# Four of twelve modulation sums accumulated on GpSimd instead of VectorE

## The chip, the cores and the metric

One core of a Trainium2 chip runs the whole program: two layers of an attention block, then two layers of a modulated mixer block, for 256 tokens of width 2048 in float32. The metric is the device time of one execution in microseconds (us), lower is better.

## What is computed

The change is in the modulation of the second block. Each of its two layers takes a conditioning vector `c` (one row of 2048) and forms shift, scale and gate rows from a 2048 x 6144 matrix; the first layer does the same for the context with `c_ctx`:

```python
def modulation(cond, w, b, n):
    m = jax.nn.silu(cond) @ w[:, :n * D_MODEL] + b[:n * D_MODEL]
    return jnp.split(m, n, axis=-1)

for i in range(DEPTH):                       # DEPTH = 2
    sh, sc, gt = modulation(c_lat, w_ada[i], b_ada[i], 3)
    u = x * (1.0 + sc) + sh
    ...
    y = even_mixer(...) if i % 2 == 0 else odd_mixer(...)
    x = layer_norm(alpha * x + gt * y, ln_g[i], ln_b[i])
```

The even mixer is a gated linear attention with four heads (`gla_chunked`, 256 keys and 256 values per head, forwards and backwards) beside a short convolution; the odd mixer is a projection, window means with a pooled product, and an output projection. Everything is float32 in and out.

## The kernel before

**The weight stream and its split.** All large products are made of float32 weights in 504 blocks of 128 x 1024 (512 KB), loaded in order by SyncE's queue into a ring of four `stage` buffers. ScalarE writes the high part of a block (`wh`, L272), VectorE the rest (`wl<-stage,wh`, L293, one TENSOR_TENSOR), both into rings of four (`SPLITS`), and TensorE does 12 matmuls of 128 x 512 for each block (L340 to L342: high by high, low by high, high by low, for two k-tiles and two token tiles). A block's `stage` buffer is loaded again once `lo_ready` says that VectorE has read it; `wh` and `wl` are written again once `split_free` says that TensorE has used them.

**The modulation beside it.** A product with one row would waste TensorE, so each modulation sum is made as 16 steps: a block of the matrix, 128 x 1024, is brought by GpSimd's queue into `mstage` (three buffers), and one instruction adds it, times a column of `silu(c)`, into one of two accumulators `macc` (the first step of a sum only multiplies, L614, the 15 others are one SCALAR_TENSOR_TENSOR each, L617). TensorE then adds over the partitions with a product by ones, either to columns (`modulation_columns`, L1884) or, for the gates, to rows (`modulation_gate`, L2123). Semaphore `mod_sum` counts the steps; GpSimd issues the load of a unit once the step three units earlier is counted. The first four sums are made for `c` and `c_ctx` together (64 loads and 128 steps, within the first block). The other eight, sums 4 to 11 in the order of `MOD_BLOCK2`, have 16 steps each, called `mod_next(k)` with k from 0 to 127.

**Order.** Every engine's program is written out by hand. VectorE's steps stand between its split instructions:

- k 0 to 63 (sums 4 to 7): in the context projection and the key, value and query projections.
- none in the four heads of the gated linear attention, where VectorE makes the decays of eight levels (L1525 to L1533) and merges their scores (L1513), while TensorE does a weight block beside each level.
- k 64 to 66 directly after the heads, 67 to 74 in `beside_y`, 75 to 78 in the convolution stage, 79 to 95 in the output projection of the even mixer (`OUTE_MODS`; the first of them, 79, ends sum 8), 96 to 127 in the odd mixer's projection (`mod_some`).

Who waits for sums 8 to 11: the gate of the first layer is sums 7 and 8 (`modulation_gate(0, 0)` and `(0, 1)`), sum 9 is turned to columns between the two token tiles of the even output projection's last blocks, and sums 10 and 11 are the gate of the last layer (`modulation_gate(1, 0)` and `(1, 1)`). A new sum may start only when its accumulator is free: sum 8 after the columns of sum 6 (`mod_summed`), sum 9 after `modulation_gate(0, 0)` (`gt_ready` at 2), sum 10 after `modulation_gate(0, 1)` (`gt_ready` at 4), sum 11 after the columns of sum 9.

Of the kernel before, what the change touches and what calls it, by code (L numbers as in the profile page):

```python
# [15 lines left out]
ALU = mybir.AluOpType  # L16
# [7 lines left out]
KT = D // P  # L24
# [65 lines left out]
MOD_BLOCK1 = [(0, True), (2, True), (1, True), (3, True)]  # L90
MOD_BLOCK2 = [(8, False), (9, False), (6, False), (4, False), (5, False), (7, False), (10, False), (11, False)]
# [2 lines left out]
MOD_LAYER = sum(MOD_OPS[0:2])  # L94
MOD_COLS = [0, 2, 4, 6, 8, 9, 10, 11, 12]
MOD_UNITS = 3
WARM_FIRST, WARM_NEXT = 8, 3
OUT_PIECES = [(0, 0, 1024), (0, 1024, 1024), (1, 0, 1024), (1, 1024, 512), (1, 1536, 512)]

# [18 lines left out]
def build(nc, A, out):  # L118
    ctx = ExitStack()
    with ctx:  # L120
        def sb(name, shape, dt=F32):
            return ctx.enter_context(nc.sbuf_tensor(name, shape, dt))
# [4 lines left out]
        def sem(name):  # L127
            return ctx.enter_context(nc.semaphore(name))
# [9 lines left out]
        arena = sb("arena", [P, 15360])  # L138
        mstage = sb("mstage", [P, MOD_UNITS, 2 * COLS])
        macc = sb("macc", [P, 2, 2 * COLS])  # L140
# [7 lines left out]
        scols = sb("scols", [P, 2, KT])  # L148
# [88 lines left out]
        o_ready, o_done = sem("o_ready"), sem("o_done")  # L237
        m_full = [sem(f"mod_full{b}") for b in range(MOD_UNITS)]
        silu_c, mod_sum = sem("silu_c"), sem("mod_sum")
        mod_summed, mod_cols = sem("mod_summed"), sem("mod_cols")  # L240
# [3 lines left out]
        def once(name):  # L244

            if name not in made:
                made[name] = sem(name)
            return made[name]
# [16 lines left out]
        block = ctx.enter_context(nc.Block())  # L265
# [335 lines left out]
        def mod_op(dve, l, i, o, both, half=0):  # L601

            n = o // 2 if both else o
            w = 1 - o % 2 if both else half
            unit = KT * (2 * l + i) + n
            block, acc, col = mstage[:, unit % MOD_UNITS, :], macc[:, w, :], scols[:, 1 - o % 2 if both else 0, n:n + 1]
            if not both or o % 2 == 0:
                dve.wait_ge(m_full[unit % MOD_UNITS], 16 * (unit // MOD_UNITS + 1))
            if n == 0:
                if i in (9, 10):  # L610
                    dve.wait_ge(once("gt_ready"), 2 if i == 9 else 4)
                else:
                    dve.wait_ge(mod_summed, 2 * l + i + 1 if i < 5 else i if i < 9 else 9)
                nc.vector.tensor_scalar(acc, block, col, None, ALU.mult).then_inc(mod_sum, 1)  # L614
            else:
                dve.wait_ge(mod_sum, mod_done(l, i) + o - (1 if both else 0))
                nc.vector.scalar_tensor_tensor(out=acc, in0=block, scalar=col, in1=acc, op0=ALU.mult,  # L617
                                               op1=ALU.add).then_inc(mod_sum, 1)
# [10 lines left out]
        @block.gpsimd  # L629
        def _(pool):  # L630
            nc.gpsimd.memset(ones[:], 1.0).then_inc(k_ready, 1)

            others = [(tab[:, 0:768], A["att_tab"]), (rope_t, A["rope"]), (bcols[:], A["bcols"]),
                      (sinks[:], A["sinks"].partition_broadcast(P)), (rcnt[:], A["rcnt"])]
            pool.wait_ge(full[3], 16)
            done = []
            for cp, both in MOD_SEQ:
                for n in range(KT):
                    unit = len(done)
                    if unit == MOD_UNITS:  # L640
                        for dst, src in others:
                            pool.dma_start(dst, src).then_inc(tables_loaded, 16)
                    if unit >= MOD_UNITS:
                        pool.wait_ge(mod_sum, done[unit - MOD_UNITS])
                    k = n % KPB
                    pool.dma_start(mstage[:, unit % MOD_UNITS, :].rearrange("p (c n) -> p c n", c=2),  # L646
                                   WM[n // KPB, :, 2 * cp:2 * cp + 2, COLS * k:COLS * k + COLS])\
                        .then_inc(m_full[unit % MOD_UNITS], 16)
                    done.append((done[-1] if done else 0) + (2 if both else 1))


        @block.scalar
# [473 lines left out]
        def _(dve):  # L1126
# [241 lines left out]

            def mod_next(k):

                i = len(MOD_BLOCK1) + k // KT
                mod_op(dve, 0, i, k % KT, False, half=i % 2)

# [76 lines left out]
            for m in range(16):  # L1450
                n = 4 * (m // 8) + m % 4
# [28 lines left out]
            for hd in range(GH):  # L1480
# [9 lines left out]
                for d, dst in ((0, PF), (1, SB_)):  # L1490
                    n = 8 + 2 * hd + d
# [25 lines left out]
                for v, b in enumerate(LEVELS + [P, None]):  # L1517
                    k = 9 * hd + v
# [343 lines left out]
        def _(pe):  # L1862
# [494 lines left out]
            def turn_quad(q, t):  # L2357

                pe.wait_ge(once("ln_first"), 2 * t + q + 1)
                _, m = u.take()  # L2360
                turned(pe, m - 2)
                for j in range(4):
                    a = P * (4 * q + j)
                    last = nc.tensor.transpose(quad(m)[0][:, P * j:P * j + P], X[:, t, a:a + P], ident[:])
                last.then_inc(tp_ready, 1)
                uses.append(u.n)
# [182 lines left out]
```

## Time and profile before

| | |
|---|---|
| three runs, median (lowest to highest) | 1728.97 us (1727.98 to 1729.22) |
| the profiled execution, its own time | 1727.48 us |
| its span in the trace | 1725.7 us |
| TensorE's mean granted clock | 0.99 of full |
| busy: TensorE, VectorE, ScalarE, GpSimd | 98%, 77%, 52%, 8% |
| moved from HBM and back | 385 MB and 4 MB, 226 GB/s over the span |

The profiled execution lies 1.5 us under the median of the three runs. Busy time of an engine is the sum of its instructions' durations; for TensorE the ends are modelled, so that its 98% does not mean peak speed. GpSimd's 8% is the issuing of transfers, 0.72 us for each. Times of stretches are given in us from the start of the span: the four heads are at 998 to 1203, the rest of the even mixer's products up to the convolution at 1203 to 1290, the end of the convolution and the even output projection at 1290 to 1396, the odd mixer's projection at 1410 to 1600.

### The profile page before, as it was taken

To read this page: it belongs to the slowest core of one execution; us is meant where nothing else is said; L and a number is where in the kernel's file an instruction comes from. 1 tells how busy PE (TensorE), PEld (TensorE's weight loads), DVE (VectorE), ACT (ScalarE), POOL (GpSimd) and SP (SyncE) were. 2 spreads that over 40 slices of the span, in tenths; PEclk is the share of its full clock that TensorE was granted. 3 is DMA by queue.
4 is the path that set the end of the run, shared out by engine and by line. 5 is a ranking of instruction groups with operands and counts; after the bars stand their busy time and mean duration, and the time that the engine had idled before them with its cause. 6 is when DMAs were issued, how large, how long until landed. Compare 5 with 4: busy or idle time off the path is not lost.

```text
span 1725.7 us, 22328 instructions
## 1 busy us (share of the span) xinstructions
PE 1684.4 (98%) x8100; PEld 1393.9 (81%) x8100; DVE 1336.4 (77%) x1805; ACT 890.8 (52%) x1353; POOL 142.0 (8%) x202
## 2 busy tenths in 40 slices
PE   9999999999999999999999999999999999999996
PEld 7888888888888888878877878778777778878885
DVE  7978878879778878687966877778876978667766
ACT  6447564455465734555844456655534364444432
POOL 1100000001000000011211200000101101110000
PEclk9999999999999999999999999999999999999998
DMA  8856545658655545689977933334959869887663
GB/s 322 328 200 205 173 160 160 205 192 305 230 183 183 173 156 195 236 279 357 336 253 228 359 118 122 123 123 147 326 183 332 306 233 318 280 260 228 223 203 111
DMA packets 110466, 390.60 MB, mean 226 GB/s; under 512 B 16204, under 2 KB 17116, under 8 KB 108732
## 3 DMA queue, kind: packets, MB, share of 16 engines
q1 hardware_dynamic: 74944, 268.99, 44.6%
q0 software_dynamic: 27856, 101.19, 19.0%
q10 hardware_dynamic: 7566, 19.08, 3.1%
q8 instruction: 64, 1.05, 0.3%
q14 instruction: 36, 0.29, 0.0%
HBM read 385.02 MB, written 4.19 MB: 226 GB/s over the span
## 4 chain that ended last, share of the span: by engine, by line
PE 84%; DVE 8%; ACT 4%; issue 2%; DMA 2%; ACTq 0%; SPq 0%; DVEq 0%
PE L L340 23%; PE L L342 23%; PE L L341 23%; PE TP L444 3%; DVE wl L293 2%; DMA stage<-in_w_stream 1%; PE AB L1884 1%; PE AB L1976 1%; ACT wh L272 1%; PE TP L1989 1%; PE AB L2281 1%; PE AB L2212 1%; PE AB L1979 1%; DVE arena L1525 1%; PE AB L1980 1%
## 5 line engine op out<-in xcount | busy, mean ns | idle before, releaser
L340 PE MATMUL L<-wh,xth 128*128 128x512 f32 (+1 forms) x1948 | 788.6, 405 | 8.7 <-DVE wl L293 5.9
L293 DVE TENSOR_TENSOR wl<-stage,wh 128x1024 fp32r<-128x1024 f32 x504 | 612.0, 1220 | 228.1 <-ACT wh L272 227.1
L272 ACT ACTIVATE wh<-stage 128x1024 fp32r<-128x1024 f32 x504 | 530.0, 1057 | 495.3 <-PE L L342 352.8
L342 PE MATMUL L<-wh,xtl 128*128 128x512 f32 (+1 forms) x1948 | 762.1, 391 | 0.0
L341 PE MATMUL L<-wl,xth 128*128 128x512 f32 (+1 forms) x1948 | 761.0, 391 | 0.0
L340 PEld LDWEIGHTS L<-wh,xth 128*128 128x128 f32 x1948 | 368.3, 189 | 86.4 <-DVE wl L293 10.2
L342 PEld LDWEIGHTS L<-wh,xtl 128*128 128x128 f32 x1948 | 367.8, 189 | 78.3
L341 PEld LDWEIGHTS L<-wl,xth 128*128 128x128 f32 x1948 | 368.6, 189 | 74.5 <-issue 4.1
L617 DVE SCALAR_TENSOR_TENSOR macc<-mstage,scols,macc 128x1024 f32<-128x1024 f32 x240 | 306.8, 1278 | 4.8 <-DMA mstage<-in_w_mod 4.0
L646 POOL DMA_DIRECT2D mstage<-in_w_mod x192 | 138.9, 723 | 1435.8 <-DVE macc L617 1002.3
L716 ACT ACTIVATE pa<-pa,st 128x128 f32<-128x128 f32 x96 | 43.1, 450 | 71.3 <-DVE st L1227 36.5
L949 ACT ACTIVATE arena<-arena 128x256 f32<-128x256 f32 (+1 forms) x136 | 48.1, 424 | 47.9 <-DVE arena L1533 47.8
L728 ACT ACTIVATE pa<-TP 128x384 f32<-128x384 f32 x48 | 23.5, 490 | 68.7 <-PE TP L1989 68.7
L444 PE MATMUL TP<-ident,arena 128*128 128x128 f32 x344 | 49.2, 275 | 1.3 <-DVE xtl L478 1.0
L444 PEld LDWEIGHTS TP<-ident,arena 128*128 128x128 f32 x344 | 41.9, 143 | 10.2 <-issue 2.5
L1218 DVE SCALAR_TENSOR_TENSOR pa<-tab,AB 128x384 f32<-128x384 f32 x48 | 26.5, 552 | 24.2 <-PE AB L1980 18.9
L1247 DVE SCALAR_TENSOR_TENSOR arena<-AB,st,arena 128x64 f32<-128x64 f32 (+1 forms) x96 | 25.0, 302 | 19.1 <-PE AB L2002 18.1
L691 ACT ACTIVATE arena<-L,st 128x512 f32<-128x512 f32 (+1 forms) x60 | 37.5, 678 | 2.0 <-PE L L342 1.9
L466 ACT ACTIVATE xth<-TP 128x512 fp32r<-128x512 f32 x40 | 23.1, 588 | 22.5 <-PE TP L444 22.5
L478 DVE TENSOR_TENSOR xtl<-TP,xth 128x512 fp32r<-128x512 f32 x40 | 27.0, 684 | 6.5 <-ACT xth L466 6.5
L2265 PEld LDWEIGHTS AB<-arena 128*128 128x128 f32 x160 | 19.9, 191 | 12.2 <-issue 6.0
L2265 PE MATMUL AB<-arena 128*128 128x128 f32 x160 | 22.2, 282 | 6.6 <-DVE arena L1493 4.8
(233 smaller groups left out, 1325.8 us busy)
## 6 DMA issues: line engine op xcount, KB each, us to landing
stage<-in_w_stream SPq DMA_DIRECT2D x504, 512.0 KB, 4.7
mstage<-in_w_mod POOLq DMA_DIRECT2D x192, 512.0 KB, 6.3
arena<-in_ctx ACTq DMA_DIRECT2D x1, 2048.0 KB, 12.9
x_kept<-X ACTq DMA_DIRECT2D x1, 2048.0 KB, 9.9
X<-x_kept ACTq DMA_DIRECT2D x1, 2048.0 KB, 11.7
arena<-in_b_ada ACTq DMA_DIRECT2D x2, 1024.0 KB, 11.3
arena<-in_ln_g ACTq DMA_DIRECT2D x2, 1024.0 KB, 9.8
X<-in_x SPq DMA_DIRECT2D x3, 512.0 KB, 8.7
```

What stands on the lines that cost most here:

```text
L272: nc.scalar.activation(wh[:, s % SPLITS].rearrange("p a b -> p (a b)"), stage[:, s % RING, :], ACT.Copy).then_inc(hi_ready, 1)
L293: nc.vector.tensor_tensor(wl[:, s % SPLITS].rearrange("p a b -> p (a b)"), stage[:, s % RING, :], wh[:, s % SPLITS].rearrange("p a b -> p ...
L340: nc.tensor.matmul(o, xh, w[0], start=start, stop=False, skip_group_check=True)
L341: nc.tensor.matmul(o, xh, w[1], start=False, stop=False, skip_group_check=True)
L342: last = nc.tensor.matmul(o, xl, w[0], start=False, stop=True, skip_group_check=True)
L444: last = nc.tensor.transpose(bank[0:width, j, t * P:t * P + P], src(t), ident[:])
L617: nc.vector.scalar_tensor_tensor(out=acc, in0=block, scalar=col, in1=acc, op0=ALU.mult, op1=ALU.add).then_inc(mod_sum, 1)
L646: pool.dma_start(mstage[:, unit % MOD_UNITS, :].rearrange("p (c n) -> p c n", c=2), WM[n // KPB, :, 2 * cp:2 * cp + 2, COLS * k:COLS * k + ...
L691: ins = nc.scalar.activation(dst(t), L[bank][:, t, 0:width], fn, scale=scale(t))
L716: ins = nc.scalar.activation(pr[b][:, a:a + w], pr[b][:, a:a + w], ACT.Exp, bias=ngm[:, 2 * b + t:2 * b + t + 1], scale=1.0 if swa else ML ...
L949: return nc.scalar.activation(dst, src, ACT.Exp, scale=1.0 / 16)
L2265: last = nc.tensor.matmul(bank[:, P * j:P * j + P], ks[:, dc, P * j:P * j + P], qs[:, dc, P * i:P * i + P], start=dc == 0, stop=dc == 1)
```

## The change

Steps k of 64 and above (sums 8 to 11) are left out of VectorE's program. GpSimd makes each of them with two instructions instead of one: it multiplies the staged block by its column in place, waits for that, and adds it to the accumulator (the first step of a sum multiplies straight into the accumulator). Its own steps stand in its program ahead of the load that needs their buffer. The places where TensorE waits, the buffers, and all loads are the same.

```diff
+POOL_MODS = 64
...
+            def pool_step(k, done):
+
+                i, n = len(MOD_BLOCK1) + k // KT, k % KT
+                unit = 4 * KT + k
+                block, acc, col = mstage[:, unit % MOD_UNITS, :], macc[:, i % 2, :], scols[:, 0, n:n + 1]
+                pool.wait_ge(m_full[unit % MOD_UNITS], 16 * (unit // MOD_UNITS + 1))
+                if n == 0:
+                    if i in (9, 10):
+                        pool.wait_ge(once("gt_ready"), 2 if i == 9 else 4)
+                    else:
+                        pool.wait_ge(mod_summed, i if i < 9 else 9)
+                pool.wait_ge(mod_sum, done[unit - 1])
+                if n == 0:
+                    nc.gpsimd.tensor_scalar(acc, block, col, None, ALU.mult).then_inc(mod_sum, 1)
+                else:
+                    nc.gpsimd.tensor_scalar(block, block, col, None, ALU.mult).then_inc(once("mod_scaled"), 1)
+                    pool.wait_ge(once("mod_scaled"), k - POOL_MODS - (k - POOL_MODS) // KT)
+                    nc.gpsimd.tensor_tensor(acc, acc, block, ALU.add).then_inc(mod_sum, 1)
...
+                    step = unit - 4 * KT - MOD_UNITS
+                    if step >= POOL_MODS:
+                        pool_step(step, done)
                     if unit >= MOD_UNITS:
                         pool.wait_ge(mod_sum, done[unit - MOD_UNITS])
...
+            for step in range(len(MOD_BLOCK2) * KT - MOD_UNITS, len(MOD_BLOCK2) * KT):
+                pool_step(step, done)
...
             def mod_next(k):
 
+                if k >= POOL_MODS:
+                    return
                 i = len(MOD_BLOCK1) + k // KT
```

GpSimd's program before, from its tables to its end (`stage_full3` is the first weight blocks' arrival, `mod_sum` the count of steps made):

```order
L631 MEMSET ones 128x128
L646 DMA mstage<-in_w_mod 128x2x512 [waits stage_full3]
L646 DMA mstage<-in_w_mod 128x2x512 x2
L642 DMA tab<-in_att_tab 128x768
L642 DMA rcnt<-in_rcnt 128x8
L646 DMA mstage<-in_w_mod 128x2x512 [waits mod_sum] x189
```

And now, from the last row before its steps on (lines are those of the changed program, in which L669 is the load; `mod_full` is the arrival of a unit in each of the three buffers, `mod_scaled` counts the scalings):

```order
L669 DMA mstage<-in_w_mod 128x2x512 [waits mod_sum] x128
L649 ISA
L649 TENSOR_SCALAR macc<-mstage,scols 128x1024 [waits mod_sum,mod_summed,mod_full2]
L669 DMA mstage<-in_w_mod 128x2x512 [waits mod_sum]
L651 TENSOR_SCALAR mstage<-mstage,scols 128x1024 [waits mod_sum,mod_full0]
L653 TENSOR_TENSOR macc<-macc,mstage 128x1024 [waits mod_scaled]
```

After 131 loads GpSimd alternates between a step (scaling and addition) and a load. The first of its steps waits for the columns of sum 6 and for nothing in the heads.

VectorE's program before, from the last instruction of the last head (L1515) on:

```order
L1515 COPY pa<-AB 128x256 [waits at_added,lv_ready]
L293 TENSOR_TENSOR wl<-stage,wh 128x1024 [waits hi_ready] x4
L614 TENSOR_SCALAR macc<-mstage,scols 128x1024 [waits mod_summed,mod_full2]
L617 SCALAR_TENSOR_TENSOR macc<-mstage,scols,macc 128x1024 [waits mod_sum,mod_full0]
L617 SCALAR_TENSOR_TENSOR macc<-mstage,scols,macc 128x1024 [waits mod_sum,mod_full1]
L538 TENSOR_SCALAR st<-st 128x8 [waits stat_sum]
L541 RECIPROCAL st<-st 128x8 [waits stat_sd]
L293 TENSOR_TENSOR wl<-stage,wh 128x1024 [waits hi_ready]
L617 SCALAR_TENSOR_TENSOR macc<-mstage,scols,macc 128x1024 [waits mod_sum,mod_full2]
```

And now (L294 is the split, which was L293, and L1542 the copy):

```order
L1542 COPY pa<-AB 128x256 [waits at_added,lv_ready]
L294 TENSOR_TENSOR wl<-stage,wh 128x1024 [waits hi_ready] x4
L539 TENSOR_SCALAR st<-st 128x8 [waits stat_sum]
L542 RECIPROCAL st<-st 128x8 [waits stat_sd]
L294 TENSOR_TENSOR wl<-stage,wh 128x1024 [waits hi_ready] x5
L1587 SCALAR_TENSOR_TENSOR arena<-arena,st,pa 128x256 [waits stat_rs,gla_w]
```

The steps between the splits are gone; the splits and all else stand in their old order, in this stretch and in the later ones.

## Rows read from the trace of the kernel before

**Rows 1.** The page: engines' busy time, then costly groups and issues.

```profile
PE 1684.4 (98%) x8100; PEld 1393.9 (81%) x8100; DVE 1336.4 (77%) x1805; ACT 890.8 (52%) x1353; POOL 142.0 (8%) x202
L617 DVE SCALAR_TENSOR_TENSOR macc<-mstage,scols,macc 128x1024 f32<-128x1024 f32 x240 | 306.8, 1278 | 4.8 <-DMA mstage<-in_w_mod 4.0
mstage<-in_w_mod POOLq DMA_DIRECT2D x192, 512.0 KB, 6.3
```

**Rows 2.** Busy time by stretch; behind POOL: granted clock, DMA share, GB/s.

```profile
998.00:1203.00 205.00, 196.87 (x1005) 163.06 (x1004) 169.44 (x306) 123.60 (x222) 0.45 (x1) 0.99 0.36 118
1203.00:1290.00 87.00, 85.28 (x363) 66.99 (x362) 65.59 (x66) 41.79 (x58) 8.22 (x12) 1.00 0.75 257
1290.00:1396.00 106.00, 101.92 (x458) 81.95 (x458) 83.93 (x88) 40.10 (x44) 14.45 (x20) 1.00 0.90 319
1410.00:1600.00 190.00, 190.00 (x841) 153.28 (x840) 137.69 (x126) 91.83 (x113) 20.96 (x29) 1.00 0.82 270
```

**Rows 3.** VectorE in order of time, one level of the second head.

```profile
1067.66 1.21 DVE L293 TENSOR_TENSOR wl<-stage,wh 128x1024 fp32r<-128x1024 f32 x1
1069.22 0.42 DVE L1525 TENSOR_TENSOR arena<-arena 128x256 f32<-128x256 f32 x1
1070.51 0.68 DVE L1529 TENSOR_TENSOR arena<-arena 128x512 f32<-128x512 f32 x1
1071.78 1.22 DVE L293 TENSOR_TENSOR wl<-stage,wh 128x1024 fp32r<-128x1024 f32 x1
```

**Rows 4.** TensorE in order of time, the same level's matmuls and the next's.

```profile
1067.79 1.05 PE L2265 MATMUL AB<-pa 128*128 128x128 f32 x8
1071.42 1.05 PE L2265 MATMUL AB<-arena 128*128 128x128 f32 x8
```

**Rows 5.** GpSimd in order of time: last load before, first after the heads.

```profile
989.42 0.72 POOL L646 DMA_DIRECT2D mstage<-in_w_mod  x1 [1.99 <-DVE macc L617]
1202.55 0.72 POOL L646 DMA_DIRECT2D mstage<-in_w_mod  x1 [212.40 <-DVE macc L614]
```

**Rows 6.** When the columns of sum 6 are read, and VectorE's first level.

```profile
996.99 0.17 DVE L624 SCALAR_TENSOR_TENSOR mcols<-AB,bcols 128x8 f32<-128x8 f32 x1 [2.04 <-PE AB L1884]
1009.73 0.42 DVE L1525 TENSOR_TENSOR arena<-arena 128x256 f32<-128x256 f32 x1 [1.08 <-ACT arena L949]
```

**Rows 7.** The modulation instructions on VectorE by stretch.

```profile
1203.00:1290.00 87.00, 13.45 (x11) 1.00 0.75 257
1290.00:1396.00 106.00, 24.30 (x19) 1.00 0.90 319
1396.00:1600.00 204.00, 38.35 (x30) 0.99 0.78 258
```

**Rows 8.** TensorE's waits, 1203 to 1290 (first row) and 1290 to 1405.

```profile
PE L L340 <- DVE wl L293: 1.3, 1, 1.3
...
PE L L340 <- DVE wl L293: 3.0, 2, 1.8
PE L L340 <- DVE xtl L1752: 2.7, 1, 2.7
PE TP L444 <- DVE xtl L478: 1.0, 1, 1.0
```

**Rows 9.** GpSimd's own instructions on data, all at the start.

```profile
L631 POOL MEMSET ones<- 128x128 f32 x1 | 0.2, 204 | 0.3 <-POOLq L2537 0.3
L2537 POOL MEMSET const-float32-0.0<- 128x1 f32 x1 | 0.1, 93 | 0.3 <-issue 0.3
```

**Rows 10.** The split's durations: min, median, max over all 504.

```profile
L293 DVE TENSOR_TENSOR wl<-stage,wh x504: 1193/1220/1229, 8.0 to 1702.9; 128x1024 fp32r<-128x1024 f32 x168
```

**Rows 11.** The chain that ended last, 1290 to 1651, of longer pieces.

```profile
1289.13 1.72 PE AB L2123 x4
...
1307.59 12.27 DMA stage<-in_w_stream
...
1322.37 12.73 DMA stage<-in_w_stream
...
1345.49 1.72 PE AB L2123 x4
1393.49 1.68 PE AB L1884 x16
...
1635.60 1.72 PE AB L2123 x4
1650.97 1.72 PE AB L2123 x4
```

## The prediction

> **What bounds the kernel now.** I read the page first. TensorE is busy for 98% of the span and VectorE for 77% [rows 1]. That says only that VectorE's relief is worth little on the whole; what it is worth is settled in the stretches where instructions leave or come. So next the busy times by stretch [rows 2], then TensorE's waits there [rows 8], then the order of time in the heads [rows 3, 4], where the change brings a new user of time.
>
> In the stretches that lose VectorE work (1203 to 1600) TensorE hardly waits for VectorE: 1.3 us up to 1290, then 3.0 us for the split, 2.7 us and 1.0 us for other instructions up to 1405 [rows 8]; from 1410 to 1600 it is busy for 190.0 of 190 us [rows 2]. In the heads it is otherwise. One level takes VectorE from 1067.66 to 1071.78, 4.12 us, and in it every instruction stands right behind the last [rows 3]. TensorE's part of a level needs 3.63 us (1067.79 to 1071.42, in a level where its blocks were ready) [rows 4]. So within the levels VectorE sets the pace and has 0.49 us too much per level: anything that holds VectorE there holds the kernel.
>
> **The change, part by part.**
>
> Removed from VectorE: 64 steps, 60 of them at 1278 ns [rows 1] and four cheaper first steps, together 13.5, 24.3 and 38.4 us in the three stretches [rows 7], 76.1 us (of them 0.7 us for each first step is not counted by that line). What of it lies on the path is bounded by what TensorE waits: at most 1.3 + 3.0 + 1.0 = 5.3 us of [rows 8] can go, since the 2.7 us end a chain of ScalarE and VectorE work without a step in it. The 3.0 us have a second cause: in 1290 to 1396 the chain holds two weight loads of 12.27 and 12.73 us [rows 11] while the transfers run at 319 GB/s with the DMA engines busy for 0.90 [rows 2]. Sum 8's 16 loads, 8 MB, move into the heads, where they run at 118 GB/s, so the pressure at 1203 to 1290 falls, but at 1290 to 1396 GpSimd still wants 16 to 19 loads where 20 were issued. I take a gain of **2 us**, between 0 and 5.3.
>
> Added to GpSimd: 64 scalings and 60 additions of 128 x 1024, and their waits. No row shows such an instruction. The nearest are two memsets: 204 ns for 128 columns and 93 ns for one [rows 9], 0.87 ns per column, hence 0.98 us for one stream of 1024 columns. A scaling is one stream in and one out: 0.98 us if they overlap, 1.87 us if not. An addition has two in: 1.87 us if only the output overlaps, 2.77 us if nothing does. I take 1.0 us for the scaling, by the memset, and the middle, 2.3 us, for the addition: 3.3 us per step (ends 2.85 and 4.6 us). The Trainium skill (GPSIMD Engine Reference, Performance versus the Vector engine) gives 4497 ns for an addition of 2048 float32 columns, thus an estimate of 2.25 us for 1024; no row here shows it, and with it the sum below would be the same to a few us.
>
> Moved: sum 8. Before, GpSimd waited 212.40 us, all through the heads, for VectorE's first step of it [rows 5]. Now its steps need only the columns of sum 6, which are there at 997.0 [rows 6]. So 16 scalings and 15 additions run in the heads. Nobody needs the sum before 1345 [rows 11]. The cost of this part is nothing if GpSimd and VectorE do not disturb each other, and at most the whole time of GpSimd's instructions, 16 x 1.0 + 15 x 2.3 = 50.5 us, if one stops while the other reads. The trace can't decide between them: GpSimd's 192 load issues leave the split's duration as it is (1193 to 1229 ns in all 504) [rows 10], but they read no tile. I take the upper kind: both engines read 128-partition tiles of the same memory, and an engine either has its own way to them or takes turns; a middle needs a special reason. The Trainium skill (SBUF — State Buffer, Who interferes with whom) states just this: a VectorE instruction with two SBUF inputs contends with a GpSimd instruction that reads SBUF, and whoever comes second is fully blocked. No run here shows it yet; by that rule the forecast stands, without it the first rival.
>
> With turns, a step takes GpSimd 3.3 us, 0.72 us for its load issue [rows 5], and about 0.5 us before each of the two while a VectorE instruction of 0.42 to 1.22 us [rows 3] ends: some 5 us, of which VectorE has 1.8 us. From 997.0 to the first level at 1009.73 [rows 6] go 2.5 steps, mostly beside VectorE's waits. The other 13.5 fall into levels that are full: 13.5 x 3.3 = 44.6 us. The 13.5 x 1.8 us of VectorE work done meanwhile are 6 levels, whose slack of 0.49 us gives back 3 us. Heads: **+42 us**, and 0 at the other end, or 60 us with 4.6 us per step. The loads cost nothing: a unit is asked for two steps ahead, 10 us, and lands in 6.3 us [rows 1].
>
> Between 1203 and 1290 GpSimd stands, since sum 9 waits for the gate product at 1289 [rows 11].
>
> From 1290 to 1396: sum 9. GpSimd's tiles take 50.5 us; VectorE keeps 83.9 - 25.0 (19 steps and a first one) = 59 us [rows 2, 7], most of it the 33 splits: 109 us wanted where there are 106. The splits have a lead of some blocks, but a split that comes late also puts off the next weight load, and those are on the chain here [rows 11]. I take +8 us, between -3 and +22.
>
> From 1396 to 1600: sums 10 and 11. GpSimd's tiles take 101 us; VectorE keeps 98 of 190 us (137.7 less the 30 steps and two first ones) [rows 2, 7]. With turns that are 1 us longer beside splits, a step takes 6.5 us: 32 of them end near 1396 + 208 = 1604 plus what was lost, and the gate wants them at 1636 and 1651 [rows 11]. TensorE has a lead of three blocks here. I take 0, and +15 if GpSimd's step is of the long kind.
>
> Sum: -2 + 42 + 8 = **+48 us** on the profiled execution's 1727.5 us, which is 1775 us; the median of the runs shown is 1.5 us above that execution, which does not matter at this size.
>
> **Rivals.**
>
> 1. *No disturbance: faster.* If the two engines read side by side, VectorE's levels stay at 4.12 us, and only the gain is left: 2 us, up to 5.3. Time 1724 us (1721 to 1729). It decides by a point that the sum gives: the loss outweighs the gain as soon as GpSimd holds VectorE for over 5.3 / 50.5, a tenth, of its own instructions' time in the heads. For it speaks that nothing in the trace shows a disturbance; against it, that the loss needs so little. Chance 0.20.
>
> 2. *GpSimd is late.* With 4.6 us per step, or if GpSimd is the one that is mostly blocked, sum 9 needs 16 x 7.5 = 120 us where 106 are, and TensorE waits at the columns at 1393 [rows 11] for 14 us; sums 10 and 11 need 240 us from there and are late for the gates by some 10 us more. If it is late by long instructions that hold VectorE too, the heads add 60: 1727.5 + 60 + 24 + 10 = 1821 us. Chance 0.12. If it is GpSimd alone that is held, only its lateness counts, about 1750 us: chance 0.08, together with a half disturbance (a slower rate instead of turns), which gives the same +24.
>
> 3. *The change does less than it says:* sum 8 does not run in the heads. Its waits are met at 997 [rows 6], so I give that nothing of its own.
>
> **How the numbers follow.** Forecast 0.60 (1755 to 1800), rival 1 0.20, late and long 0.12, held or half 0.08. A measurement of this kernel tells about 0.2%, 3.5 us, from no change. Rival 1 lies across that border: 0.12 faster, 0.08 same. All else is slower: 0.80. The range for 8 in 10 has to reach from the edge of rival 1 to the lower part of the long case: 1726 to 1812 us.
>
> **What would show it.** In the changed profile: GpSimd's scaling near 1.0 us and addition near 2.3 us when alone; in the heads 16 of each but one, from 997 on; the split and the level instructions there longer than 1.22 and 0.42 to 0.68 us, or gaps between them, as long as GpSimd works, and levels of 4.12 us as soon as it has ended; the first head longer by some 40 us and the last unchanged. From 1410 on splits that are longer without TensorE waiting. The prediction is wrong if the levels beside GpSimd's steps keep 4.12 us (rival 1), or if TensorE waits at the columns of sum 9 or at the last gate (rival 2).

## The result and the profile after

The changed kernel takes 1776.63 us (median of 4 runs, 1772.02 to 1782.21) against 1728.47 us before (1726.06 to 1729.22): 1.028 times, interval 1.0263 to 1.0297. It is 48 us slower. Its profiled execution has a span of 1773.7 us, 48.0 us over the 1725.7 us before.

First the page of the changed kernel: busy time, and the groups that answer to [rows 1]; behind the bar busy us, mean ns of one, and the idle time before them. L294 is the split (L293 before).

```profile
PE 1701.7 (96%) x8100; PEld 1404.9 (79%) x8100; DVE 1374.8 (78%) x1741; ACT 891.3 (50%) x1353; POOL 509.1 (29%) x326
...
L294 DVE TENSOR_TENSOR wl<-stage,wh 128x1024 fp32r<-128x1024 f32 x504 | 673.8, 1347 | 230.9 <-ACT wh L273 229.3
...
L618 DVE SCALAR_TENSOR_TENSOR macc<-mstage,scols,macc 128x1024 f32<-128x1024 f32 x180 | 230.0, 1278 | 6.4 <-DMA mstage<-in_w_mod 6.0
L651 POOL TENSOR_SCALAR mstage<-mstage,scols 128x1024 f32<-128x1024 f32 x60 | 192.8, 3214 | 2.9 <-POOL macc L653 0.3
L653 POOL TENSOR_TENSOR macc<-macc,mstage 128x1024 f32<-128x1024 f32 x60 | 158.7, 2644 | 5.0
```

VectorE makes 60 of these instructions fewer and is busy for 38 us more. Its records have grown: an instruction that is held back counts as busy. The split's mean went from 1220 to 1347 ns, while its shortest is still 1192 ns.

The next view is VectorE in order of time within the first head, one level of the changed kernel, to be read against [rows 3]; columns are start, duration, engine, line, operation.

```profile
1023.24 1.21 DVE L294 TENSOR_TENSOR wl<-stage,wh 128x1024 fp32r<-128x1024 f32 x1
1024.38 0.44 DVE L1540 COPY_PREDICATED pa<-tab,AB 128x256 f32<-128x256 uint32 x1
1024.80 0.92 DVE L1552 TENSOR_TENSOR arena<-arena 128x256 f32<-128x256 f32 x1
1025.64 0.41 DVE L1553 TENSOR_TENSOR arena<-arena 128x256 f32<-128x256 f32 x1
1025.98 0.68 DVE L1555 TENSOR_TENSOR arena<-arena 128x512 f32<-128x512 f32 x1
1026.58 0.68 DVE L1556 TENSOR_TENSOR arena<-arena 128x512 f32<-128x512 f32 x1
1027.18 0.41 DVE L1559 TENSOR_TENSOR arena<-arena 128x256 f32<-128x256 f32 x1
1027.52 2.60 DVE L1560 TENSOR_TENSOR arena<-arena 128x256 f32<-128x256 f32 x1
1030.04 1.21 DVE L294 TENSOR_TENSOR wl<-stage,wh 128x1024 fp32r<-128x1024 f32 x1
```

And GpSimd in the same time:

```profile
1023.33 0.77 POOL L669 DMA_DIRECT2D mstage<-in_w_mod  x1 [0.30 <-POOL macc L653]
1024.14 3.03 POOL L651 TENSOR_SCALAR mstage<-mstage,scols 128x1024 f32<-128x1024 f32 x1
1027.25 2.58 POOL L653 TENSOR_TENSOR macc<-macc,mstage 128x1024 f32<-128x1024 f32 x1
1030.13 0.77 POOL L669 DMA_DIRECT2D mstage<-in_w_mod  x1 [0.30 <-POOL macc L653]
```

L1560 wants 0.42 us. It starts 0.27 us after GpSimd's addition and ends at 1030.12, 0.29 us after the addition's end at 1029.83: held for nearly all of it. L1552 meets the scaling and is 0.92 us long in place of 0.43; but L1553 to L1556 run at full speed while the scaling goes on until 1027.17. A level takes 6.80 us (1023.24 to 1030.04) against 4.12 us: 2.2 us for the addition, 0.5 us for the scaling.

How much a scaling costs depends on when VectorE's instruction comes. In the second head the same L1556 starts just behind a scaling and takes 1.64 us in place of 0.68:

```profile
1092.09 2.86 POOL L651 TENSOR_SCALAR mstage<-mstage,scols 128x1024 f32<-128x1024 f32 x1
1092.12 1.64 DVE L1556 TENSOR_TENSOR pa<-arena 128x512 f32<-128x512 f32 x1
```

If it needs its usual 0.68 us once it is let in, it was let in 1.0 us after the scaling's start (an estimate from these two rows: 1092.12 + 1.64 - 0.68 - 1092.09). The same working over the whole profile, for the 34 scalings that were not lengthened themselves: all 13 splits and level instructions that started in their first 0.98 us were held, and let in 0.98 to 1.02 us after the scaling's start; none of the 34 that started later was held. In the additions that were not lengthened the 24 held instructions were let in 2.19 to 2.30 us after the start. So a scaling keeps these instructions out for about the first 1.0 us of its 2.86, an addition for about 2.3 of its 2.4 us. The page calls GpSimd's spans rough, but these numbers hardly vary.

In the levels of the second head the scaling costs 1.0 us so, and the addition 1.7 us (L1552 takes 2.17 us); a level takes 6.8 us again. TensorE waits for the levels (first the two rows of the changed kernel, then the same two of the kernel before):

```profile
PE AB L2292 <- DVE pa L1556: 16.2, 10, 2.9
PE AB L2292 <- DVE arena L1556: 7.3, 11, 1.4
...
PE AB L2265 <- DVE arena L1529: 1.7, 9, 0.2
PE AB L2265 <- DVE pa L1529: 1.0, 5, 0.2
```

(TensorE's waits over the whole execution: us in total, times, longest.) Not every instruction of VectorE is held. In the view by line, which gives min/median/max in ns, those with two inputs in the on-chip memory have long ones; those that read the matmuls' memory (`TP`, `AB`, `L`) and at most one tile of the on-chip memory have none, nor has the memset:

```profile
L1560 DVE TENSOR_TENSOR arena<-arena x32: 410/417/2605, 1016.1 to 1224.8; 128x256 f32<-128x256 f32 x32
...
L1540 DVE COPY_PREDICATED pa<-tab,AB x28: 430/440/450, 1024.4 to 1225.2; 128x256 f32<-128x256 uint32 x28
...
L1515 DVE MEMSET arena<- x4: 485/485/485, 1001.4 to 1188.1; 128x512 f32 x4
...
L479 DVE TENSOR_TENSOR xtl<-TP,xth x40: 676/682/692, 239.2 to 1677.5; 128x512 fp32r<-128x512 f32 x40
...
L1697 DVE TENSOR_TENSOR arena<-L,arena x8: 678/682/693, 1370.1 to 1443.4; 128x512 f32<-128x512 f32 x8
```

The Trainium skill (SBUF — State Buffer, Who interferes with whom) says that an instruction with two SBUF inputs contends with a GpSimd instruction that reads SBUF and that one with at most one, outside VectorE's two-port modes, does not: these rows agree, with 2605 ns beside 417 and 450 beside 440. For how long they contend is another matter, as the scaling shows.

To place the 48 us I use one ruler for all kernels, the starts of the same instructions: the first and the fourth head's scaling of queries (L1486 before), the first gate product, the last product for the columns of sum 9, the last low part of the turned tiles at the start of the odd mixer (L1752 before), the last gate product, and the end. Lengths in us between them, each from one profiled execution; the part ahead of the heads varies from 995.6 to 1003.2 us in all these executions and is left out.

| kernel | heads 1 to 4 | to the gate | sum 9 | between the mixers | odd mixer | end |
|---|---|---|---|---|---|---|
| before | 158.3 | 132.8 | 105.9 | 18.6 | 238.6 | 73.6 |
| changed | 187.4 | 132.8 | 113.0 | 25.3 | 241.7 | 73.6 |
| e1, sum 8 only | 187.1 | 132.7 | 102.0 | 20.3 | 238.5 | 73.6 |
| e2, sums 9 to 11 | 156.7 | 132.8 | 136.8 | 24.3 | 242.0 | 73.6 |
| e3, sums 10 and 11 | 158.1 | 132.9 | 105.4 | 24.1 | 241.7 | 73.6 |
| e4, VectorE's steps narrow | 158.9 | 132.8 | 104.8 | 17.4 | 238.6 | 73.6 |
| e5, scalings alone | 161.7 | 132.7 | 115.5 | 20.9 | 239.4 | 73.6 |
| e6, additions alone | 190.8 | 132.8 | 138.6 | 32.6 | 250.2 | 73.5 |
| e7, writes alone | 158.8 | 132.8 | 104.4 | 19.1 | 238.6 | 73.6 |
| e8, GpSimd's steps narrow | 158.1 | 132.8 | 107.2 | 18.8 | 238.5 | 73.6 |
| e9, sum 11 only | 159.0 | 132.8 | 104.5 | 17.4 | 238.7 | 73.6 |
| e10, sum 10 late | 189.0 | 132.8 | 114.9 | 20.6 | 245.1 | 73.5 |
| e11, additions apart | 185.4 | 132.7 | 112.5 | 25.3 | 250.4 | 73.6 |

The changed kernel loses 29.1 us in the heads (19.9 in the first, 9.3 in the second, nothing in the third), 7.1 with sum 9, 6.7 between the mixers and 3.1 in the odd mixer: 46.0 us, and 2.0 us lie ahead of the heads.

With sum 9 TensorE stands before the columns for 2.8 us and then works at half the clock, so that the product itself takes 3.57 us in place of 1.68 [rows 11]. Its timeline there, in the changed kernel:

```profile
1426.74 0.39 PE L343 MATMUL L<-wh,xtl 128*128 128x512 f32 x1
1429.90 3.57 PE L1911 MATMUL AB<-ones,macc 128*128 128x1 f32 x16 [2.77 <-POOL macc L653]
1433.34 0.77 PE L341 MATMUL L<-wh,xth 128*128 128x512 f32 x1
```

GpSimd's last addition for the sum, the 15th, ended at 1429.85; it had started the sum at 1322.16, 6.7 us per step. Between the mixers, VectorE normalizes in a chain that TensorE waits for. The view is VectorE in order of time:

```profile
1438.77 2.16 DVE L1724 SCALAR_TENSOR_TENSOR st<-moments,st 128x1 f32<-128x1 f32 x1
1440.97 2.46 DVE L1772 TENSOR_SCALAR X<-X,st 128x512 f32<-128x512 f32 x2
```

In the kernel before these were 0.16 and 1.00 us:

```profile
1399.20 0.16 DVE L1697 SCALAR_TENSOR_TENSOR st<-moments,st 128x1 f32<-128x1 f32 x1
1399.40 1.00 DVE L1745 TENSOR_SCALAR X<-X,st 128x512 f32<-128x512 f32 x2
```

One column costs 2 us when it meets an addition (GpSimd's record: 1437.86 to 1440.92). The pair on `X` meets a scaling: its second instruction takes 2.00 us and starts at 1441.43, while GpSimd still issues a load (1441.21 to 1441.98); the scaling's record begins at 1442.02, and the instruction is let in 0.9 us after that, by the working above. So it was held from before the record of what holds it.

TensorE has little to do meanwhile, and its clock falls. First the stretch with the product for sum 9's columns, then the stretches after the norm, of the changed kernel (busy time of TensorE, its weight loads, VectorE, ScalarE, GpSimd, then granted clock, DMA share, GB/s):

```profile
1429.90:1433.50 3.60, 3.60 (x17) 3.60 (x18) 1.60 (x4) 0.00 (x0) 3.31 (x2) 0.50 0.51 159
...
1441.10:1445.10 4.00, 1.77 (x8) 1.13 (x8) 3.93 (x5) 2.14 (x5) 3.76 (x3) 0.80 0.49 157
1445.10:1449.10 4.00, 1.10 (x3) 0.94 (x4) 3.79 (x7) 2.95 (x7) 3.66 (x3) 0.50 0.04 6
1449.10:1453.10 4.00, 4.00 (x11) 3.07 (x10) 3.96 (x6) 1.64 (x3) 3.92 (x2) 0.50 0.83 242
```

0.50 is the lower level, 1.2 GHz; in the last stretch TensorE is busy throughout and does 11 matmuls where it does some 20 at the upper level. In the kernel before, the clock falls here too, but less: 0.64 from 1403 to 1407 us and 0.94 in the next 4 us.

### The profile page after: what moved, and what is told of

Same layout as the page of the kernel before. It is cut to its first block, busy times and chain, and to the rows that moved or that the text cites. A ratio compares the mean times of both kernels' runs of the same rounds, so it can differ in the third digit from the quotient of the medians.

```text
span 1773.7 us, 22391 instructions
## 1 busy us (share of the span) xinstructions
PE 1701.7 (96%) x8100; PEld 1404.9 (79%) x8100; DVE 1374.8 (78%) x1741; ACT 891.3 (50%) x1353; POOL 509.1 (29%) x326
## 4 chain that ended last, share of the span: by engine, by line
PE 69%; issue 14%; DVE 7%; POOL 6%; ACT 3%; DMA 1%; ACTq 0%; DVEq 0%; POOLq 0%
PE L L341 19%; PE L L343 19%; PE L L342 19%; POOL mstage L651 3%; PE TP L445 3%; POOL macc L653 2%; PE AB L1911 1%; PE AB L2003 1%; DVE wl L294 1%; DVE arena L1560 1%; DMA arena<-in_w_gate 1%; PE TP L2016 1%; DVE arena L1552 1%; PE AB L2239 1%; ACT wh L273 1%
## 5 line engine op out<-in xcount | busy, mean ns | idle before, releaser
L294 DVE TENSOR_TENSOR wl<-stage,wh 128x1024 fp32r<-128x1024 f32 x504 | 673.8, 1347 | 230.9 <-ACT wh L273 229.3
L669 POOL DMA_DIRECT2D mstage<-in_w_mod x192 | 141.8, 739 | 913.1 <-DVE macc L618 708.7
L618 DVE SCALAR_TENSOR_TENSOR macc<-mstage,scols,macc 128x1024 f32<-128x1024 f32 x180 | 230.0, 1278 | 6.4 <-DMA mstage<-in_w_mod 6.0
L651 POOL TENSOR_SCALAR mstage<-mstage,scols 128x1024 f32<-128x1024 f32 x60 | 192.8, 3214 | 2.9 <-POOL macc L653 0.3
L653 POOL TENSOR_TENSOR macc<-macc,mstage 128x1024 f32<-128x1024 f32 x60 | 158.7, 2644 | 5.0
L649 POOL TENSOR_SCALAR macc<-mstage,scols 128x1024 f32<-128x1024 f32 x4 | 12.8, 3189 | 223.5 <-issue 216.4
L1272 DVE SCALAR_TENSOR_TENSOR arena<-AB,st,arena 128x64 f32<-128x64 f32 (+1 forms) x96 | 25.0, 302 | 19.1 <-PE AB L2029 18.1
L2292 PE MATMUL AB<-pa 128*128 128x128 f32 x128 | 21.0, 314 | 16.3 <-DVE pa L1556 16.2
```

Source lines behind the costliest of these rows:

```text
L294: nc.vector.tensor_tensor(wl[:, s % SPLITS].rearrange("p a b -> p (a b)"), stage[:, s % RING, :], wh[:, s % SPLITS].rearrange("p a b -> p ...
L651: nc.gpsimd.tensor_scalar(block, block, col, None, ALU.mult).then_inc(once("mod_scaled"), 1)
L653: nc.gpsimd.tensor_tensor(acc, acc, block, ALU.add).then_inc(mod_sum, 1)
```

## The experiments

The theory: GpSimd and VectorE take turns at reading, and this costs time where TensorE waits for VectorE soon. Rivals: the loss comes from GpSimd being late for TensorE; from the new order of loads and waits; from any GpSimd work on tiles, reading or not.

**e1: sum 8 alone on GpSimd.** In the changed kernel:

```diff
-                    if step >= POOL_MODS:
+                    if POOL_MODS <= step < POOL_MODS + KT:
...
-                if k >= POOL_MODS:
+                if POOL_MODS <= k < POOL_MODS + KT:
                     return
+                if k == POOL_MODS + KT:
+                    dve.wait_ge(mod_sum, mod_done(0, 9))
```

and without the last loop over `pool_step`.

> GpSimd makes sum 8 alone, in the heads; VectorE makes sums 9 to 11 as before. Theory (the two engines take turns, and the heads pay because VectorE is full there): in the change's profile the starts of the first and the fourth head lie 29 us further apart than before, so this kernel is 27 to 31 us above the kernel before, 1755 to 1760 us, and everything from the end of the heads on has its old length. Rival (most of the 48 us come after the heads, from GpSimd being late for TensorE): under 1745 us.

Measured 1755.95 us, 1.0149 (1.0133 to 1.0165) times before. The heads are 28.8 us longer; of the rest, sum 9's stretch is 3.9 us shorter and the one between the mixers 1.7 us longer in this profile. The largest part of the loss is this one sum in the heads.

**e2 and e3: sums 9 to 11, and 10 and 11, on GpSimd.**

```diff
-POOL_MODS = 64
+POOL_MODS = 80
```

and 96 for e3.

> VectorE makes sum 8 as before, GpSimd sums 9 to 11, so nothing of GpSimd runs in the heads. Theory: the heads are as before, and what is left of the change's 48 us is 17 to 19 us, 1744 to 1748 us; with the run of sum 8 alone the two add up to the change's. Rival (late for TensorE): 30 us or more are left here, over 1757 us.

> VectorE makes sums 8 and 9, GpSimd 10 and 11 alone. In the change's profile the stretch in which sum 9 runs is 7 us longer than before and TensorE waits 6 us in it for GpSimd's last addition at the columns. If that wait is all that stretch costs, this kernel is 7 us under the run of sums 9 to 11, at 1737 to 1741 us, and the rest, 9 to 12 us, is VectorE held in the odd projection. Rival (sums 10 and 11 cost nothing, since TensorE sets the pace there): 1728 us, as before.

e2 gave 1771.19 us, 1.0247 (1.0231 to 1.0262): 23 us over the range expected; the rival's number is met. Its waits of TensorE say why:

```profile
PE AB L1911 <- POOL macc L653: 28.3, 1, 28.3
```

(The profiled execution has a time of 1763.62 us, 7.6 us under the median, so the table holds less than the whole loss.) In e2 GpSimd may start sum 9 only once VectorE has ended sum 8, and that is far on in the output projection:

```profile
1309.93 2.85 POOL L649 TENSOR_SCALAR macc<-mstage,scols 128x1024 f32<-128x1024 f32 x1
```

There are 24.8 us from the gate product (1285.1) to this; in the changed kernel 2.1 us (1320.1 to 1322.16). The heads are as before (156.7), and sum 9's stretch is 30.9 us longer. So the parts don't add: with sum 8 out of the way early, GpSimd just about meets the columns, and without that it is the bound. e3 gave 1737.46 us, 1.0047 (1.0032 to 1.0062), 9.3 us over its kernel before: 5.5 us between the mixers and 3.1 in the odd mixer. That lies in the range expected, but not by the reasoning given for it: e3 is 34 us under e2 and not 7, and most of its loss is in the stretch between the mixers. The 6 us that the expectation names for the wait at the columns are 2.8 us of the matmuls and 3.2 us of the weight loads, which pass side by side; TensorE stood for 2.8 us.

**e4: what the relief of VectorE is worth.** In the kernel before, in `mod_op`:

```diff
+            if unit >= 8 * KT:
+                block, acc = block[:, 0:8], acc[:, 0:8]
```

> The kernel before, with VectorE's steps of sums 8 to 11 made on 8 of the 1024 columns: VectorE is relieved of 64 steps, nothing goes to GpSimd, loads and waits stay. The other 1016 columns of these sums are left out. This is the most that the move can give. The prediction took 2 us of it, at most 5.3: 1723 to 1728 us. If it gives over 8 us, the gain was undersized and the loss with it.

Measured 1729.66 us, 0.9998 (0.9989 to 1.0008): nothing, and just over the range expected. Taking the 64 steps from VectorE gives no time where they stand.

**e5 to e8: which part of a step costs.** In `pool_step`, e5 keeps the scaling of a step without the addition, e6 the addition without the scaling; e7 has five memsets in place of both, e8 cuts every step to 8 columns. First e8's edit, then e7's:

```diff
+                block, acc = block[:, 0:8], acc[:, 0:8]
```

```diff
-                    nc.gpsimd.tensor_scalar(block, block, col, None, ALU.mult).then_inc(once("mod_scaled"), 1)
-                    pool.wait_ge(once("mod_scaled"), k - POOL_MODS - (k - POOL_MODS) // KT)
-                    nc.gpsimd.tensor_tensor(acc, acc, block, ALU.add).then_inc(mod_sum, 1)
+                    for m in range(5):
+                        nc.gpsimd.memset(block, 0.0).then_inc(once("mod_scaled"), 1)
+                        pool.wait_ge(once("mod_scaled"), 5 * (k - POOL_MODS - (k - POOL_MODS) // KT - 1) + m + 1)
+                    pool.sem_inc(mod_sum, 1)
```

> The change without its 60 additions (they are left out; the scalings in place, the loads and all waits stay). In the change's profile a level instruction of VectorE that meets a scaling is about 0.5 us longer, one that meets an addition 2.2 us. Theory (a scaling keeps VectorE out for a part of its 2.86 us only, an addition for all of its 2.4 us): the heads are 8 to 15 us longer, 1734 to 1745 us in all. Rival (each GpSimd instruction keeps VectorE out for its whole time): 16 x 2.86 = 46 us in the heads, over 1765 us. Other rival (only additions disturb): 1728 us.

> The change without its 60 scalings in place: the block is added as it is (the scaling is left out). Theory: 15 additions of 2.4 us in the heads, each holding VectorE for about 2.2 us, 30 us there, and a few after: 1758 to 1768 us. If the two parts simply add, this and the run with scalings alone together lose about the change's 48 us. Rival (the scaling is the costly half): under 1745 us.

> In place of each scaling and addition GpSimd makes five memsets of the same block (the sums are left out), by the 0.98 us estimated for one about 5 us of GpSimd time per step, as long as scaling and addition, but nothing is read. Theory (what they take turns for is reading): the level instructions in the heads keep 0.42 and 0.68 us, 1726 to 1731 us. Rival (any GpSimd work on tiles holds VectorE): 1770 us or more.

> The change with every GpSimd step made on 8 of the 1024 columns: the same instructions, waits, loads and order, and hardly any reading (the other 1016 columns of these sums are left out). Theory (the 48 us are the time of the two instructions' reading, and the lateness that comes from their length): as before, 1724 to 1731 us. Rival (the new order of loads, the extra waits or the code that GpSimd loads costs something): over 1735 us.

e7: 1728.59 us, 0.9998 (0.9983 to 1.0012). GpSimd is busy beside the levels as in the change, with 300 memsets of 0.96 us, and VectorE does not notice:

```profile
L652 POOL MEMSET mstage<- 128x1024 f32 x300 | 287.9, 960 | 14.3 <-POOLq L654 0.4
```

e8: 1729.23 us, 1.001 (0.9997 to 1.0022), with the same instructions, loads and waits as the change. So neither writing nor the order costs. What is left is the part that both runs lack: GpSimd's reading of 1024 columns. Since e8 also moves sum 8's loads into the heads, as the change does, it shows too that the whole move, without that reading, gains nothing.

e5: 1747.02 us, 1.0108 (1.0086 to 1.013), 2 us over the range expected. The heads lose 3.4 us, less than I expected; most of the loss is with sum 9 (9.6 us), where TensorE waits 9.6 us for late splits, 3.0 us before. Without additions a step takes 4 us instead of 6.7, so that 27 scalings fall into that stretch, 17 in the change. VectorE and GpSimd in e5, one level and one step:

```profile
1027.95 1.21 DVE L294 TENSOR_TENSOR wl<-stage,wh 128x1024 fp32r<-128x1024 f32 x1
1029.09 0.45 DVE L1538 COPY_PREDICATED pa<-tab,AB 128x256 f32<-128x256 uint32 x1
1029.50 0.92 DVE L1550 TENSOR_TENSOR arena<-arena 128x256 f32<-128x256 f32 x1
...
1032.55 1.21 DVE L294 TENSOR_TENSOR wl<-stage,wh 128x1024 fp32r<-128x1024 f32 x1
```

```profile
1028.37 3.50 POOL L651 TENSOR_SCALAR mstage<-mstage,scols 128x1024 f32<-128x1024 f32 x1
```

The scaling is 3.50 us long instead of 2.86 (it waits for the split, which ends at 1029.16), and L1550 loses 0.5 us in it; all later instructions of the level run free. L1550 is let in at 1029.99, 1.0 us after the scaling would have started by its length: the same 1.0 us as in the change.

e6: 1820.66 us, 1.0532 (1.0511 to 1.0552). This is the great miss: 92 us, more than scalings and additions together. Its heads lose 32.5 us, as expected; but the stretch of sum 9 loses 32.7, and the two after it 25.6. A part of this is pace: without scalings a step takes 3.4 us, sum 10 starts before sum 9's stretch has ended, and 30 additions fall into it, 15 in the change. TensorE waits 20.8 us for splits there. In the heads one sees how closely the additions stand:

```profile
1020.56 2.35 POOL L651 TENSOR_TENSOR macc<-macc,mstage 128x1024 f32<-128x1024 f32 x1
1023.21 0.72 POOL L667 DMA_DIRECT2D mstage<-in_w_mod  x1 [0.30 <-POOL macc L651]
1023.95 2.38 POOL L651 TENSOR_TENSOR macc<-macc,mstage 128x1024 f32<-128x1024 f32 x1
```

```profile
1016.67 3.40 DVE L1553 TENSOR_TENSOR arena<-arena 128x512 f32<-128x512 f32 x1
1020.00 3.47 DVE L1554 TENSOR_TENSOR arena<-arena 128x512 f32<-128x512 f32 x1
1023.39 3.23 DVE L1557 TENSOR_TENSOR arena<-arena 128x256 f32<-128x256 f32 x1
```

Each of these three instructions of VectorE takes nearly a whole period of 3.4 us, though the addition is 2.4 us long. L1554 starts at 1020.00, while GpSimd still issues a load (1019.81 to 1020.53) and 0.56 us before the addition's record begins, and yet it is held.

**e11: additions alone, apart from the loads.** The load's issue is followed by a memset of 8 columns of a tile of its own, for whose end the addition waits. Against the changed kernel:

```diff
-                    nc.gpsimd.tensor_scalar(block, block, col, None, ALU.mult).then_inc(once("mod_scaled"), 1)
+                    nc.gpsimd.memset(mark[:], 0.0).then_inc(once("mod_scaled"), 1)
```

> The run with additions alone, with a memset of 8 columns between the issue of the load and the addition, whose end the addition waits for (the scalings are left out). In the run with additions alone only one instruction of VectorE gets through per 3.4 us, though an addition takes 2.4 us: theory, the next addition takes the read side while the load is still being issued. Then this run lets VectorE through for some 0.7 us more per step, VectorE's instructions beside it are held for 2.4 us at most in place of 2.8, and the time falls from 1820.7 us to 1785 to 1805 us. Rival (the gap of a load's issue is lost to VectorE for another reason): 1815 us or more.

Measured 1781.11 us, 1.0306 (1.0291 to 1.0322), 40 us less than e6, for two extra things to do per step: a little more than expected. The split now gets through in the gap at full speed, and the held ones are 2.1 to 2.6 us long:

```profile
1018.30 2.60 DVE L1560 TENSOR_TENSOR arena<-arena 128x256 f32<-128x256 f32 x1
1020.82 0.41 DVE L1561 TENSOR_TENSOR arena<-arena 128x256 f32<-128x256 f32 x1
1021.16 1.21 DVE L295 TENSOR_TENSOR wl<-stage,wh 128x1024 fp32r<-128x1024 f32 x1
1022.78 2.08 DVE L1553 TENSOR_TENSOR arena<-arena 128x256 f32<-128x256 f32 x1 [0.42 <-ACT arena L975]
```

This is what one would see if GpSimd's next reading instruction, when nothing holds it back, takes the read side during the issue before it; the pair on `X` in the changed kernel fits this as well. That it does so is my reading; no record shows the taking itself, and GpSimd's records may begin late. Nor does e11 separate the gap from the pace: a step takes 3.6 to 4.1 us in it, 3.4 in e6, and 24 additions fall into sum 9's stretch in place of 30. The heads have 15 additions in both, and there e11 is only 5.4 us shorter.

**e9: sum 11 alone, in the middle of the odd mixer** (`POOL_MODS = 112`).

> GpSimd makes sum 11 alone, from about 1500 us on, where TensorE is busy without a break; VectorE makes the rest as before. Theory (a held VectorE costs only where TensorE waits for it soon): within 3 us of the kernel before, 1726 to 1731 us, with splits of up to 3 us in the stretch and no wait of TensorE for them. Rival (each step costs its part of the 9.3 us of sums 10 and 11): 4.5 us above, 1733 us.

Measured 1726.86 us, 0.9994 (0.9983 to 1.0006). Splits are up to 3.42 us long, 0.4 us more than expected, and TensorE waits for none from 1480 us on:

```profile
L294 DVE TENSOR_TENSOR wl<-stage,wh x504: 1194/1220/3418, 8.3 to 1704.5; 128x1024 fp32r<-128x1024 f32 x168
```

The same 31 instructions that cost 28 us in the heads (e1) cost nothing here: it is the place that makes the price.

**e10: the change with sum 10 started late.**

```diff
+                    if i == 10:
+                        pool.wait_ge(once("ln_first"), 4)
```

> The change, with sum 10 started only when VectorE has scaled its columns of the normed rows (one more wait on GpSimd), so that nothing of GpSimd runs in the short stretch between the even and the odd mixer. By the stretches of the profiles that one is 25.3 us in the change, 20.3 us in the run of sum 8 alone and 18.6 us before. Theory: 5 us less than the change, 1770 to 1773 us; the steps come about 20 us later and still end before the gate wants them. Rival (the held time only moves, or the gates wait): 1776 us or more.

Measured 1772.66 us (5 runs), 1.0261 (1.0247 to 1.0275) of its kernel before, 4 us under the change's median; the intervals of the two ratios overlap, so the runs alone don't prove a gain. The stretches show it: the one between the mixers falls from 25.3 to 20.6 us, as said, and 3.4 us are lost again in the odd mixer, which was not expected.

Since e4 and e8 find nothing to gain from the move, I expect no version of it to beat the kernel before; the best measured, e9, equals it.

## Why the prediction was right

The forecast was 1775 us and the measurement 1776.63 us, by the mechanism named, and the heads carry the most of it. But the terms are off by up to 13 us and cancel: that the total agrees to 2 us is luck.

**The bound, right.** VectorE full in the levels, with 0.49 us of slack: a level takes 2.68 us more now, and 29 of the 48 us are in the heads. e1 shows it alone. As soon as GpSimd's last addition has ended (1104.65), a level takes 4.1 us again (the splits at 1107.06 and 1111.17), as the prediction said.

**Turns, right, but only for reading.** The upper end was taken from two bounds without a row between them. e7 and e8 leave the reading as what costs, and the profile after shows that it is VectorE's instructions with two inputs in the on-chip memory, and the `TENSOR_SCALAR` on `X`, that are held.

**The term "heads +42 us" was too large: 29.1 us.** The step that failed is the count of 13.5 steps in full levels, and the step time of 5 us beneath it, which comes from "I take 1.0 us for the scaling, by the memset". A scaling takes 2.86 us, over even the upper end of 1.87 us; the addition takes 2.4 us, near the 2.3 us taken. So a step comes every 6.8 us, nearly once per level, and the 16 steps reach from 999.11 to 1104.65, over the change from the first head to the second. By GpSimd's records two steps start before the first level, seven in the levels of the first head, four between the heads (1058 to 1082), where VectorE waits for others anyway, and three in the second head: 10 in full levels in place of 13.5, at 2.7 us each in place of 3.3. That is 27 of the 29.1 us. The prediction had the whole loss in the first head; it is 19.9 and 9.3 us.

The premise that an instruction is shut out for the whole of the other's time, which the prediction also cites, holds nearly for the addition (2.3 of 2.4 us) and fails for the scaling (1.0 of 2.86 us). Had it held, the longer scaling would have cost far more. That the time for which a scaling shuts VectorE out is the 1.0 us that the prediction took for its whole length is luck too. Of these 3.3 us per step a level loses 2.7, since the first part of each passes beside an instruction that already runs or that is not held.

**The term "-2 us", a gain: 0.** e4 gives 0.9998, e8 1.001. The 5.3 us of waits for VectorE [rows 8] do not go when its steps go, so they end on something else; the table gives 1.1 us for sum 9 and 1.2 us between the mixers in e4, within what such stretches vary.

**Sum 9, "+8 us": 7.1 us, for the most part for another reason.** I expected late splits. But TensorE stood before the columns until GpSimd itself had ended, which needs 107.7 us (1322.16 to 1429.85) for the 106 us that there are: the mechanism of rival 2 in a mild form. The prediction had named this wait as a sign that it is wrong, and in this stretch it was. The wait is 2.8 us of the 7.1, and the product at half the clock 1.9 us; the other 2.4 us are not placed. The length of the scaling is again the cause: with 1.0 us, a step would be 1.9 us shorter. e2 shows how near the edge this was: GpSimd starts 23 us later after the gate product, and TensorE waits 28.3 us.

**Sums 10 and 11, "0": 9.8 us.** e3 has 9.3 us. The stretch between the mixers was not looked at in the prediction: it is 19 us long, a chain of short VectorE instructions with TensorE waiting, and GpSimd's steps fall into it. There a held instruction costs its whole time and some clock beside it. In the odd mixer proper, where I argued with TensorE's lead, the cost is 3.1 us, of which TensorE waits 2.6 us for VectorE near its end (none before), and nothing for sum 11 alone (e9).

Taken together: 42 - 29.1 = 12.9 us too much in the heads and 0.9 too much with sum 9; 9.8 us too little behind, 2 us of gain that there was not, and 2 us that vary ahead of the heads. Two numbers of the rivals don't follow from their own text: 1727.5 less a gain of 2 us is 1725.5 us and not 1724, and the 1821 us of rival 2 add 10 us for the gates that its 24 us already hold. What stays open is the 3.4 us that e10 loses again in the odd mixer, when exactly GpSimd takes the read side, and why a scaling frees it after 1.0 us of 2.86.

## What to carry to other kernels

Before work is moved to GpSimd, look at what VectorE does beside it, not only at how busy both are: an addition of 1024 float32 columns held back a VectorE instruction for 2.0 to 2.2 us whether that had 1024 columns or one, and it cost all of that in a chain (heads, norm) and nothing under the matmul stream of the odd mixer (e9). Measure first what the relief gives, by making the moved instructions narrow where they stand; here it was zero. A helper that is slower than the engine it replaces also needs its own time against each place that waits for it: 16 steps of 6.7 us against 106 us.

## What the runs showed that was not expected

- A float32 scaling in place of 128 x 1024 takes GpSimd 2.86 us, longer than an addition of two such tiles (2.34 to 2.40 us when undisturbed), yet it keeps VectorE's two-input instructions out only for its first 1.0 us, the addition for 2.3 us. Of this the levels of the first head see 0.5 and 2.2 us, those of the second 1.0 and 1.7 us.
- Additions that follow a load's issue directly cost more than the same additions with a scaling between (e6, 1820.66 us, against the change, 1776.63 us): VectorE got one instruction through per 3.4 us. A wait on a memset of 8 columns took 40 us off (e11). Pace has a share in both, as said there.
- GpSimd's memsets of 128 x 1024 (0.96 us each, 300 of them) slowed nothing (e7).
- A VectorE instruction on one column (0.16 us) took 2.16 us beside an addition, and a `TENSOR_SCALAR` with a single input tile (0.5 us for 512 columns) was held as well, by a scaling: the pair took 2.46 us in place of 1.00. The Trainium skill (SBUF — State Buffer, Who interferes with whom) counts `tensor_scalar` in a two-port mode among those that contend; the row agrees, though no row shows in which mode it ran.
